# First transformer block on one core: the pool projections and the first gates in another order

## The chip, the core and the metric

The kernel runs on one core of one Trainium2 chip. The metric is the device time of one execution in microseconds (us), as the median of the runs shown. The engines are TensorE (PE, its weight loads apart as PEld), VectorE (DVE), ScalarE (ACT), GpSimd (POOL) and the SyncE queue (SP), which issues DMAs.

## What is computed

Two transformer blocks in sequence on 512 tokens of width 1024, in float32. The change lies in the first one, whose mixer has two branches:

```python
z = u @ w_in[l]                       # pool part, q, k, v, two gates
win_sum = cs[:, 1:, sl] - cs[:, lo, sl]
outs.append(win_sum / count - pf[:, :, sl])      # per group, windows (2, 4, 8, 16)
y = jnp.einsum('bsgc,gcd->bsgd', y, pool_w)      # one 128x128 matrix per group
y = y.reshape(B, S, POOL_WIDTH) * pool_scale
y_pool = pool_mixer(p, pool_w[l], pool_scale[l]) @ w_branch_pool[l]
y_attn = moba_attention(q, k, v) @ w_branch_attn[l]
m = jax.nn.sigmoid(g_pool) * y_pool + jax.nn.sigmoid(g_attn) * y_attn
```

## The kernel before

All activations lie transposed, 128 features by 512 tokens a tile. A float32 product is made of three matmuls of rounded parts: weight high by input high (L397), weight high by input low (L401), weight low by input high (L405). So each weight block of 128x128 costs three matmuls of 512 columns, and each operand is made in two steps: a high part (ACT, `round`, L293, or L285 for weights) and the rest, the low part (POOL, L245 or L241 for weights, or DVE, L500).

The order of every engine is written out ahead of time by a planner (`Flow.run`, L907). One generator, the main line, yields the large products one after another; beside it processes wait for events that the planner reckons with its own clock (attention heads, evacuations, products of the pool). When nothing beside the main line is ripe on TensorE, the next step of the main line is issued, so the projections fill the gaps between the heads: they are the fillers of the change's name. `linear` (L1033) issues the steps of one projection: with G tiles at a time, K = 8 input tiles, G x 8 x 3 matmuls. Only where the main line itself has no step that can be issued (`yield "idle"`) does the planner resume a process that isn't ripe; on the chip that is a wait in TensorE's row.

The names, in `first_block` (L1649):

- `w_p`, three tiles in a row: the projections of pool groups 1, 2 and 3 (group 0 is done with the first products of the block), 24 matmuls each. `pool_in(g)` (L1680) takes the result: evacuation from PSUM with the norm's factor (`scaled_out`, DVE, L646), g + 1 doublings that make a window's sum (`double`, DVE, L675 and the copy L676), the mean (`mean`, DVE, L681, L683, L684), high part on ACT (L293), low part on POOL (L245).
- `pool_product(g)` (L1744): three matmuls (L483, L484, L485) with the group's matrix, the scale (DVE, L691), high part (ACT, L293), low part (DVE, L500). The matrices come with one DMA (`pool_weights`, L1732, L208).
- `w_gp` and `w_ga`: the gates of the pool and of the attention, here the first two tiles of each, 48 matmuls a pair; evacuated (L646) and put through a sigmoid (L347).
- `w_bp`: the branch product of the pool. It reads the results of groups 0, 1, 2, 3 in this order, six matmuls a group for two tiles. `w_ba` follows, the branch product of the attention.

In the kernel before the main line runs: the last q, k, v tiles, then `w_p` for groups 1, 2, 3, then `w_gp`, `w_ga`, then `w_bp`. The attention's last two heads (6 and 7) are issued among the `w_p` steps: `turn` (L427) transposes, `pv_halves` (L449, L454) products, on DVE `add_half` (L630) and `out_low` / `turn_low` (L639).

Of the kernel before, what the change touches and what calls it, by code (L numbers as in the profile page):

```python
# [140 lines left out]
class Machine:  # L141
# [32 lines left out]
    def hl(self, i):  # L174
        return self.ra[:, i, 0, :], self.ra[:, i, 1, :]

    def vc(self, name, i):
        return self.vec[:, V_COLS[name] + i:V_COLS[name] + i + 1]
# [669 lines left out]
class Schedule:  # L848
# [9 lines left out]
    def row(self, kind, *args):  # L858
        self.rows.append((kind, args))
        self.begun.append(self.time_of(args))  # L860
        return len(self.rows) - 1
# [12 lines left out]
    def done(self, engine, name, key):  # L874

        n = key[0] if isinstance(key, tuple) else key
        kind, args = self.rows[n]
        start = max(self.clock[engine], self.begun[n] + 0.06)
        took = duration(kind, engine, args)
        self.begun[n] = self.ended[(name, key)] = start + took  # L880
        self.clock[engine] = start + max(0.06, took - (0.0 if engine in ("pe", "gp") else 0.09))
        self.last[engine] = (self.m.sig(name), key)
        return self.last[engine]
# [53 lines left out]
def build(sc, m, A, out):  # L937
# [45 lines left out]
    def next_unit(name, idx):  # L983
        u = st["used"]
        st["used"] += 1
        if u % 2 == 0:
            sc.units.append((name, idx // 2))
        if plan is None:
            return u, WS[u % NU], None
        assert plan[u // 2] == (name, idx // 2), (plan[u // 2], name, idx)  # L990
        while st["split"] < min(total, u + 1 + min(LOOK, 1 + u)):
            put_split(st["split"])
            st["split"] += 1
        return u, unit_slot(u), unit_tok[u]
# [9 lines left out]
    def banks_of(lb, n):  # L1004

        if None in [bank_free[b] for b in lb[:n]]:
            return None
        bs = [rot(lb) for _ in range(n)]
        freed = tuple(tuple(bank_free[b]) for b in bs)
        for b in bs:  # L1010
            bank_free[b] = None
        return bs, freed
# [10 lines left out]
    def multiply(unit, places, x, freed, start, stop, evac=None):  # L1023

        u, parts, split_done = unit
        xh, xl, xt = x
        n = row("mm", parts, split_done, (xh, xl), high_of(xt), tuple(xt), places, freed, start, stop)
        unit_used[u] = done("pe", "mm", (n, len(places) - 1))
        if stop:
            for j, (b, _) in enumerate(places):  # L1030
                evac(j, b, (m.sig("mm"), (n, j)))

    def linear(name, G, K, rhs, ntiles, evac, lb, first=0):  # L1033

        kk = 4 // G
        base = first * K // 4
        for g in range(ntiles // G):
            got = banks_of(lb, G)
            while got is None:
                yield "idle"  # L1040
                got = banks_of(lb, G)
            bs, freed = got
            for ku in range(K // kk):
                unit = next_unit(name, base + g * (K // kk) + ku)
                for q in range(kk):
                    k = ku * kk + q
                    while rhs(k) is None:
                        yield "idle"
                    places = tuple((b, (q * G + j) * 128) for j, b in enumerate(bs))
                    multiply(unit, places, rhs(k), freed, k == 0, k == K - 1,  # L1050
                             lambda j, b, t: evac(first + g * G + j, b, t))
                    freed = ()
                    yield
# [35 lines left out]
    def parts_of(dst, src, made, eng, free, tell, scale=1.0):  # L1089

        dh, dl = dst
        yield 0, "ac", lambda: (*made, *free())
        hi = done("ac", "high", row("round", dh, src, tuple(made), tuple(free()), scale))
        yield 0, eng, lambda: (hi,)
        n = row("rest", dl, dh, src, hi, eng)
        tell(done("ve", "low_v", n) if eng == "v" else done("gp", "low_p", n))
# [21 lines left out]
    def rhs_of(x):  # L1118
        return lambda k: (*x["slots"][k], x["tok"][k]) if x["tok"][k] else None
# [45 lines left out]
    def scaled(x, b, tok, need=3):  # L1165

        yield 0, "v", lambda: (tok, x["rb"]) if x["rb"] and len(T.free) >= need else None
        i, z, free = T.get()
        v = done("ve", "evac", row("scaled_out", z, b, x["rb"], free, tok))
        bank_free[b] = stat["rb_use"] = (v,)  # L1170
        return i, z, v
# [81 lines left out]
    LB3 = [0, 1, STB]  # L1253
# [395 lines left out]
    def first_block():  # L1649
# [9 lines left out]
        rhs_u = rhs_of(u)  # L1659
# [20 lines left out]
        def pool_in(g):  # L1680
            def process(b, tok):
                i0, x, v = yield from scaled(u, b, tok, 5)
                yield 0, "v", lambda: (v,) if len(T.free) > 3 else None
                (i1, y1, f1), (i2, y2, f2) = T.get(), T.get()
                src, dst, oth, free = x, y1, y2, (*f1, *f2)
                for r in range(g + 1):
                    yield 0, "v", lambda: (v,)
                    v = done("ve", "elem_v", row("double", dst, src, 1 << r, v, free))
                    src, dst, oth, free = dst, oth, dst, ()
                yield 0, "v", lambda: (v,)  # L1690
                v = done("ve", "elem_v", row("mean", dst, src, x, g, v))

                def tell(y):
                    for i in (i0, i1, i2):
                        T.release(i, y)
                    p_in[g] = (y,)
                yield from parts_of(hl(PY + g), dst, (v,), "p", tuple, tell)
            return lambda _, b, tok: launch(process(b, tok))
# [21 lines left out]
        for j in range(1, 4):  # L1720
            gate = lambda j=j: j < 2 or 2 * j - 3 in heads_used
            for name, ev in (("w_q", qk_tile(j, 0, qs(j))), ("w_k", qk_tile(j, 1, None)),
                             ("w_v", v_tile(u, VV + j % 2, ("v", j), gate))):
                yield from linear(name, 1, 8, rhs_u, 1, ev, lb, first=j - 1)
                if lb[-1] == 5:
                    lb = LB2
        yield from linear("w_p", 1, 8, rhs_u, 3, lambda j, b, t: pool_in(j + 1)(0, b, t), LB3)

        pw_parts = hl(PT1 + 2)
        pw_tok = []  # L1730
# [13 lines left out]
        def pool_product(g):  # L1744
            yield 0, "pe", lambda: (*pw_tok, *p_in[g], *bank_free[LB7[0]]) if (
                pw_tok and g in p_in and T.free and bank_free[LB7[0]] is not None) else None
            b = rot(LB7)
            n = row("pool_mm", pw_parts, slice(128 * g, 128 * g + 128), hl(PY + g), b, (*bank_free[b], *pw_tok, *p_in[g]))
            t = done("pe", "mm", (n, 0))
            bank_free[b] = None  # L1750
            i, z, free = T.get()
            yield 0, "v", lambda: (t,)
            v = done("ve", "evac", row("pool_scale", z, b, g, t, free))
            bank_free[b] = (v,)

            def tell(y):
                T.release(i, y)
                pool_done[g] = (y,)
            yield from parts_of(hl(PY + g), z, (v,), "v", lambda: (t,), tell)
# [5 lines left out]
        def evac_g(base):  # L1765
            def f(j, b, tok):
                def process():
                    i, z, v = yield from scaled(u, b, tok, 4)
                    yield 0, "ac", lambda: (v,)
                    sg[(base, j)] = (i, z, done("ac", "act", row("sigmoid", z, vc("b_gate", base + j), v)))  # L1770
                launch(process())
            return f
# [28 lines left out]
        launch(pool_weights())  # L1801
        for g in range(4):
            launch(pool_product(g))
        yield from linear("w_gp", 2, 8, rhs_u, 2, evac_g(0), LB3, first=0)
        yield from linear("w_ga", 2, 8, rhs_u, 2, evac_g(8), LB3, first=0)
        while 7 not in heads_used:
            yield "idle"
        t_heads = now("pe")
# [467 lines left out]
    def whole():  # L2276
        u = yield from first_block()
        u = yield from second_block_diff(u)
        u, back = yield from ffn2(0, u, U_B, ("attn", 8))
        u = yield from second_block_sliding(u, back)  # L2280
        yield from ffn2(1, u, None, None)
# [127 lines left out]
```

## Time and profile before

| | |
|---|---|
| Median of 3 runs | 1958.52 us (1957.97 to 1958.56) |
| The profiled execution, its own time | 1956.75 us |
| Its span, first to last instruction | 1954.9 us |
| TensorE busy | 1930.3 us, 99% |
| DVE / ACT / POOL busy | 1176.4 / 923.8 / 1107.9 us |
| TensorE idle with a named releaser | 18.9 us in eleven kinds of wait, the longest 7.5 us at the start |
| Mean granted clock of TensorE | 0.997 |

The profiled execution lies 1.85 us above its span and 1.77 us below the median. TensorE is busy nearly all the time, so what a change does is read from the places where TensorE has nothing to issue, from the wait that ends last there, and from the granted clock behind such a place. A granted clock of 1.00 is 2.4 GHz, 0.50 is 1.2 GHz. Most stalls of the whole program are a microsecond or less.

### The profile page before, as it was taken

What the parts mean: (1) busy time and instruction counts of PE and PEld (TensorE: products, weight loads), DVE (VectorE), ACT (ScalarE), POOL (GpSimd) and SP (SyncE); (2) the same over time, 40 slices, a digit from 0 to 9 for tenths busy, and PEclk for the clock granted to TensorE, in tenths of its full rate; (3) what the DMA queues carried; (4) which work ended last, traced back from release to release, by engine and by line L of the source; (5) the groups of instructions that cost most, each with busy time, mean ns of one, the idle gap of its engine ahead of it and who ended that gap; (6) DMA issues with size and microseconds to landing.
All of it is one profiled execution on the core that took longest, in us unless ns stands there. A gap on an engine that the chain in (4) does not pass through costs nothing.

```text
span 1954.9 us, 25157 instructions
## 1 busy us (share of the span) xinstructions
PE 1930.3 (99%) x9200; PEld 1589.6 (81%) x9200; DVE 1176.4 (60%) x1978; ACT 923.8 (47%) x1752; POOL 1107.9 (57%) x848
## 2 busy tenths in 40 slices
PE   8999999999999999999999999999999999999998
PEld 6878888888888887777888888888787888888887
DVE  6773325353433488776774746756688775746755
ACT  5644336533333366554543443445577543433443
POOL 5335544454444457554675666664874576656653
PEclk9999999999999999999999999999999999999999
DMA  4122233233232332112323322323211323222321
GB/s 170 57 71 97 95 110 129 95 105 103 97 111 97 101 105 76 54 55 70 128 94 108 98 86 97 108 87 108 72 44 33 130 98 103 98 91 97 99 95 65
DMA packets 53705, 182.71 MB, mean 93 GB/s; under 512 B 5840, under 2 KB 8272, under 8 KB 53584
## 3 DMA queue, kind: packets, MB, share of 16 engines
q1 hardware_dynamic: 53584, 181.12, 28.0%
q8 instruction: 73, 1.20, 0.3%
q14 instruction: 48, 0.39, 0.1%
HBM read 174.80 MB, written 6.29 MB: 93 GB/s over the span
## 4 chain that ended last, share of the span: by engine, by line
PE 96%; DVE 3%; ACT 0%; issue 0%; DMA 0%; SPq 0%; DVEq 0%; ACTq 0%
PE b L397 29%; PE b L405 29%; PE b L401 29%; PE b L427 3%; PE b L417 1%; PE b L454 1%; PE b L465 1%; PE b L449 1%; PE b L420 1%; PE b L421 1%; PE b L475 0%; PE b L434 0%; PE b L440 0%; PE b L441 0%; DVE ra L639 0%
## 5 line engine op out<-in xcount | busy, mean ns | idle before, releaser
L241 POOL TENSOR_TENSOR ra<-raw,ra 128x512 fp32r<-128x512 f32 x632 | 876.5, 1395 | 756.9 <-ACT ra L285 755.3
L397 PE MATMUL b<-ra 128*128 128x512 f32 (+1 forms) x2560 | 890.2, 392 | 11.0 <-ACT ra L285 7.5
L405 PE MATMUL b<-ra 128*128 128x512 f32 (+1 forms) x2560 | 877.0, 387 | 0.0
L401 PE MATMUL b<-ra 128*128 128x512 f32 (+1 forms) x2560 | 876.7, 387 | 0.0
L285 ACT ACTIVATE ra<-raw 128x512 fp32r<-128x512 f32 x632 | 392.0, 628 | 521.9 <-PE b L405 513.4
L397 PEld LDWEIGHTS b<-ra 128*128 128x128 f32 x2560 | 480.9, 188 | 109.8 <-issue 10.6
L405 PEld LDWEIGHTS b<-ra 128*128 128x128 f32 x2560 | 481.0, 188 | 98.9
L401 PEld LDWEIGHTS b<-ra 128*128 128x128 f32 x2560 | 482.0, 188 | 94.0 <-DVE ra L500 0.4
L755 DVE TENSOR_TENSOR h<-b,h 128x512 f32<-128x512 f32 x136 | 91.5, 682 | 56.1 <-PE b L405 55.5
L646 DVE TENSOR_TENSOR tmp<-b,rb 128x512 f32<-128x512 f32 x66 | 45.2, 690 | 109.4 <-PE b L405 109.1
L639 DVE TENSOR_TENSOR ra<-b,ra 128x512 fp32r<-128x512 f32 (+4 forms) x166 | 92.1, 566 | 22.3 <-ACT ra L336 20.3
L646 DVE TENSOR_TENSOR gbuf<-b,rb 128x512 f32<-128x512 f32 x50 | 34.2, 689 | 99.0 <-PE b L405 99.0
L336 ACT ACTIVATE ra<-b 128x512 fp32r<-128x512 f32 (+3 forms) x142 | 66.6, 487 | 49.6 <-PE b L427 48.5
L725 DVE TENSOR_TENSOR fa<-b,fa 128x512 f32<-128x512 f32 x56 | 38.6, 688 | 78.8 <-PE b L405 78.8
L293 ACT ACTIVATE ra<-tmp 128x512 fp32r<-128x512 f32 x83 | 51.2, 627 | 57.2 <-DVE tmp L774 25.6
L500 DVE TENSOR_TENSOR ra<-tmp,ra 128x512 fp32r<-128x512 f32 x65 | 67.1, 1048 | 4.3 <-ACT ra L293 3.8
L330 ACT ACTIVATE fa<-fa,sm 128x257 f32<-128x257 f32 (+4 forms) x96 | 53.4, 558 | 23.7 <-DVE sm L617 23.3
L427 PE MATMUL b<-ident,fa 128*128 128x128 f32 x368 | 59.9, 278 | 2.8 <-DVE ra L639 2.7
L427 PEld LDWEIGHTS b<-ident,fa 128*128 128x128 f32 x368 | 41.8, 141 | 15.8 <-DVE ra L639 5.8
L592 DVE TENSOR_REDUCE sm<-b 128x1 f32<-128x512 f32 x64 | 39.8, 681 | 18.8 <-PE b L421 18.7
L506 DVE SCALAR_TENSOR_TENSOR ra<-h,vec,ra 128x512 fp32r<-128x512 f32 x40 | 44.5, 1118 | 9.0 <-ACT ra L298 9.0
L617 DVE CUSTOM_DVE_ANT_0 fa<-b,mask 128x257 f32<-128x257 f32 (+4 forms) x96 | 43.6, 486 | 6.0 <-PE b L421 5.6
(277 smaller groups left out, 1806.7 us busy)
## 6 DMA issues: line engine op xcount, KB each, us to landing
raw<-in_f_g SPq DMA_DIRECT2D x40, 512.0 KB, 3.4
raw<-in_f_v SPq DMA_DIRECT2D x40, 512.0 KB, 3.5
raw<-in_f_d SPq DMA_DIRECT2D x40, 512.0 KB, 3.4
raw<-in_w_up SPq DMA_DIRECT2D x32, 512.0 KB, 3.5
raw<-in_w_down SPq DMA_DIRECT2D x32, 512.0 KB, 3.4
raw<-in_p_g SPq DMA_DIRECT2D x16, 512.0 KB, 3.4
raw<-in_w_gp SPq DMA_DIRECT2D x8, 512.0 KB, 3.5
raw<-in_w_ga SPq DMA_DIRECT2D x8, 512.0 KB, 3.5
```

What stands on the lines that cost most here:

```text
L241: e.tensor_tensor(wl, src, wh.bitcast(F), ALU.subtract).then_inc(*w_low.mark(n))
L285: e.activation(wh, src, ACT.Copy).then_inc(*w_high.mark(n))
L330: e.activation(p, p, ACT.Exp, bias=nm, scale=-1.0, accum_out=su).then_inc(*soft.mark(n))
L336: e.activation(dst, src, ACT.Copy).then_inc(*high.mark(n))
L397: e.matmul(m.banks[b][:, 0:xh.shape[-1]], wh[:, c:c + 128], xh, start=start, stop=False)
L401: e.matmul(m.banks[b][:, 0:xh.shape[-1]], wh[:, c:c + 128], xl, start=False, stop=False)
L405: last = e.matmul(m.banks[b][:, 0:xh.shape[-1]], wl[:, c:c + 128], xh, start=False, stop=stop)
L427: x = e.transpose(m.banks[b][:, 128 * q:128 * q + 128], src[:, 128 * q:128 * q + 128], m.ident[:, :])
L500: e.tensor_tensor(dl, src, dh.bitcast(F), ALU.subtract).then_inc(*low.mark(n))
L639: e.tensor_tensor(dl, src, dh.bitcast(F), ALU.subtract).then_inc(*low.mark(n))
L646: e.tensor_tensor(z, banks[b][:, :], m.rb[:, :], ALU.mult).then_inc(*evac.mark(n))
L755: e.tensor_tensor(dst, src, hk, ALU.add).then_inc(*evac.mark(n))
```

## The change

The three tiles of `w_p` are no longer yielded in a row. Group 3 comes first, then the two gate tiles of `w_gp`, then group 2, then the two gate tiles of `w_ga`, then group 1, and then the main line goes on to `w_bp`. The processes of `pool_weights` and `pool_product` are launched ahead of the three tiles instead of behind them. Nothing is added or left out: each engine does the same operations on the same shapes.

```diff
                 yield from linear(name, 1, 8, rhs_u, 1, ev, lb, first=j - 1)
                 if lb[-1] == 5:
                     lb = LB2
-        yield from linear("w_p", 1, 8, rhs_u, 3, lambda j, b, t: pool_in(j + 1)(0, b, t), LB3)
...
         launch(pool_weights())
         for g in range(4):
             launch(pool_product(g))
-        yield from linear("w_gp", 2, 8, rhs_u, 2, evac_g(0), LB3, first=0)
-        yield from linear("w_ga", 2, 8, rhs_u, 2, evac_g(8), LB3, first=0)
+        for g in (3, 2, 1):
+            yield from linear("w_p", 1, 8, rhs_u, 1, lambda j, b, t: pool_in(j + 1)(0, b, t), LB3, first=g - 1)
+            if g > 1:
+                yield from linear(("w_ga", "w_gp")[g - 2], 2, 8, rhs_u, 2, evac_g((8, 0)[g - 2]), LB3, first=0)
```

How the rows of the engines move. A row is a line of the kernel, the operation, what it writes and reads (`b0` to `b7` are the PSUM banks, `ra` holds operands in high and low parts, `tmp` and `gbuf` are scratch tiles), its size, and in brackets the signals that it waits for: `evac` an evacuation on DVE, `mm` a product of TensorE, `high` a high part on ACT, `low_p` and `low_v` a low part on POOL and on DVE, `w_high` and `w_low_p` the two parts of weights.

TensorE before, where the last projection of `w_p` ends (bank b7, group 3):

```order
L397 MATMUL b7<-ra 128x512
L401 MATMUL b7<-ra 128x512
L405 MATMUL b7<-ra 128x512
L397 MATMUL b0<-ra 128x512 [waits evac,w_high]
L401 MATMUL b0<-ra 128x512
L405 MATMUL b0<-ra 128x512 [waits w_low_p]
L397 MATMUL b1<-ra 128x512 [waits evac]
```

Behind it stand the 96 matmuls of the gates, from b0 and b1 on, and only then the first product of the pool.

TensorE now, just behind the last matmul of the last projection (bank b0, group 1); b3 and b4 are the two tiles of `w_bp`, L483 to L485 on b5 the pool's product of group 1:

```order
L397 MATMUL b3<-ra 128x512 [waits high,w_high]
L401 MATMUL b3<-ra 128x512 [waits low_v]
L405 MATMUL b3<-ra 128x512 [waits w_low_p]
L397 MATMUL b4<-ra 128x512
L401 MATMUL b4<-ra 128x512
L405 MATMUL b4<-ra 128x512
L483 MATMUL b5<-ra 128x512 [waits low_p]
L484 MATMUL b5<-ra 128x512
L485 MATMUL b5<-ra 128x512
L397 MATMUL b3<-ra 128x512 [waits high]
L397 MATMUL b4<-ra 128x512
L401 MATMUL b3<-ra 128x512 [waits low_v]
```

Between the end of a projection and a row that needs its result there stand six matmuls where there were 96 and more.

DVE before, the chain of group 1 (from its first doubling on), then the attention's `add_half`:

```order
L675 TENSOR_TENSOR gbuf<-tmp 128x511 [waits evac,low_p]
L676 COPY gbuf<-tmp 128x1
L675 TENSOR_TENSOR gbuf<-gbuf 128x510 [waits elem_v]
L676 COPY gbuf<-gbuf 128x2
L681 TENSOR_TENSOR gbuf<-gbuf,vec 128x16 [waits elem_v]
L683 TENSOR_TENSOR gbuf<-gbuf,tmp 128x16 [waits elem_v]
L684 SCALAR_TENSOR_TENSOR gbuf<-gbuf,tmp 128x496
L630 TENSOR_TENSOR b6<-b6,ssq 64x512 [waits act]
```

DVE now, the same chain of group 1 with what stands ahead of and behind it:

```order
L500 TENSOR_TENSOR ra<-gbuf,ra 128x512 [waits high]
L500 TENSOR_TENSOR ra<-tmp,ra 128x512 [waits high]
L646 TENSOR_TENSOR tmp<-b0,rb 128x512 [waits low_p,mm]
L675 TENSOR_TENSOR tmp<-tmp 128x511 [waits evac]
L676 COPY tmp<-tmp 128x1
L675 TENSOR_TENSOR tmp<-tmp 128x510 [waits elem_v]
L676 COPY tmp<-tmp 128x2
L681 TENSOR_TENSOR tmp<-tmp,vec 128x16 [waits elem_v]
L683 TENSOR_TENSOR tmp<-tmp 128x16 [waits elem_v]
L684 SCALAR_TENSOR_TENSOR tmp<-tmp 128x496
L691 TENSOR_SCALAR gbuf<-b5,vec 128x512 [waits low_v,mm]
L500 TENSOR_TENSOR ra<-gbuf,ra 128x512 [waits high]
```

The chain of group 1 has moved behind the attention and behind the products of groups 2 and 3, whose low parts are the two rows ahead of it; its own product's scale and low part stand right behind it.

DVE now, at the place where the chain of group 1 stood before: the doublings of group 3 (third and fourth), with the last heads' rows among them:

```order
L675 TENSOR_TENSOR gbuf<-gbuf 128x508 [waits elem_v]
L676 COPY gbuf<-gbuf 128x4
L630 TENSOR_TENSOR b6<-b6,ssq 64x512 [waits act]
L675 TENSOR_TENSOR gbuf<-gbuf 128x504 [waits elem_v]
L676 COPY gbuf<-gbuf 128x8
L639 TENSOR_TENSOR ra<-b2,ra 128x128 [waits high]
L639 TENSOR_TENSOR ra<-b3,ra 128x2x128 [waits high]
L639 TENSOR_TENSOR ra<-b4,ra 128x3x128 [waits high]
L639 TENSOR_TENSOR ra<-b5,ra 128x4x128 [waits high]
```

Two doublings and two copies more stand ahead of the low parts of head 7, and the mean now behind them.

## Rows read from the trace of the kernel before

**Rows 1.** The page: busy us (share of the span) and instructions of each engine.

```profile
PE 1930.3 (99%) x9200; PEld 1589.6 (81%) x9200; DVE 1176.4 (60%) x1978; ACT 923.8 (47%) x1752; POOL 1107.9 (57%) x848
```

**Rows 2.** Waits of TensorE, whole span: us in total, times, longest.

```profile
PE b L397 <- ACT ra L285: 7.5, 1, 7.5
PE b L427 <- DVE ra L639: 2.7, 3, 1.8
PE b L397 <- DVE tmp L646: 2.0, 1, 2.0
...
PE b L397 <- ACT gbuf L353: 0.4, 1, 0.4
PE b L397 <- DVE gbuf L646: 0.2, 1, 0.2
```

**Rows 3.** A stretch: length; busy us of PE, PEld, DVE, ACT, POOL; clock; DMA.

```profile
160.00:170.00 10.00, 10.00 (x45) 7.99 (x44) 6.33 (x10) 4.60 (x8) 3.85 (x3) 1.00 0.15 52
```

**Rows 4.** TensorE timeline, group 1's projection ends: start us, us, row.

```profile
121.73 0.40 PE L405 MATMUL b<-ra 128*128 128x512 f32 x1
```

**Rows 5.** DVE timeline, group 1's chain.

```profile
122.16 0.69 DVE L646 TENSOR_TENSOR tmp<-b,rb 128x512 f32<-128x512 f32 x1
122.96 0.92 DVE L675 TENSOR_TENSOR gbuf<-tmp 128x511 f32<-128x511 f32 x1
...
123.97 0.69 DVE L675 TENSOR_TENSOR gbuf<-gbuf 128x510 f32<-128x510 f32 x1
124.58 0.16 DVE L676 COPY gbuf<-gbuf 128x2 f32<-128x2 f32 x1
...
125.08 0.67 DVE L684 SCALAR_TENSOR_TENSOR gbuf<-gbuf,tmp 128x496 f32<-128x496 f32 x1
```

**Rows 6.** ACT and POOL timelines, the end of group 1's chain.

```profile
125.97 0.65 ACT L293 ACTIVATE ra<-gbuf 128x512 fp32r<-128x512 f32 x1
...
126.70 1.29 POOL L245 TENSOR_TENSOR ra<-gbuf,ra 128x512 fp32r<-128x512 f32 x1 [3.37 <-ACT ra L293]
```

**Rows 7.** TensorE, ACT and DVE timelines, products of the pool, then `w_bp`.

```profile
159.20 0.39 PE L485 MATMUL b<-ra 128*128 128x512 f32 x1
...
161.47 0.39 PE L397 MATMUL b<-ra 128*128 128x512 f32 x1
161.82 0.50 PE L401 MATMUL b<-ra 128*128 128x512 f32 x1
...
160.41 1.32 ACT L293 ACTIVATE ra<-tmp 128x512 fp32r<-128x512 f32 x2
...
161.07 0.69 DVE L500 TENSOR_TENSOR ra<-tmp,ra 128x512 fp32r<-128x512 f32 x1
```

**Rows 8.** Timelines at the stall of 2 us: DVE, then TensorE.

```profile
111.74 0.68 DVE L646 TENSOR_TENSOR tmp<-b,rb 128x512 f32<-128x512 f32 x1
...
112.56 0.52 PE L397 MATMUL b<-ra 128*128 128x512 f32 x1 [2.01 <-DVE tmp L646]
```

**Rows 9.** Stretches of 2 us behind that stall, columns as Rows 3.

```profile
112.00:114.00 2.00, 1.44 (x5) 1.11 (x6) 1.93 (x5) 0.67 (x3) 1.28 (x1) 0.71 0.01 4
114.00:116.00 2.00, 2.00 (x10) 1.23 (x8) 0.78 (x2) 0.60 (x1) 0.00 (x0) 0.50 0.00 0
116.00:118.00 2.00, 2.00 (x11) 1.48 (x10) 1.75 (x6) 1.11 (x4) 0.00 (x0) 0.94 0.00 0
```

**Rows 10.** DVE and POOL timelines, doublings of group 3 beside POOL.

```profile
139.42 1.60 DVE L675 TENSOR_TENSOR tmp<-tmp 128x510 f32<-128x510 f32 x1
140.95 1.25 DVE L676 COPY tmp<-tmp 128x2 f32<-128x2 f32 x1
...
139.10 1.37 POOL L241 TENSOR_TENSOR ra<-raw,ra 128x512 fp32r<-128x512 f32 x1 [3.76 <-ACT ra L285]
```

**Rows 11.** DVE and TensorE timelines, last heads' low parts and head 7's product.

```profile
126.39 2.27 DVE L639 TENSOR_TENSOR ra<-b,ra 128x128 fp32r<-128x128 f32 x5
...
129.09 0.74 PE L449 MATMUL b<-ra 128*128 128x512 f32 x4
```

## The prediction, as it stood before the changed kernel ran

> **What bounds the kernel now.** I began with the busy times of the page: TensorE is busy 1930.3 us, 99% [rows 1], so an edit that adds or removes no work can change the time only where TensorE stands still or runs at the lower clock. Next I read the waits of TensorE over the whole span: eleven kinds, 18.9 us in all, led by the 7.5 us at the start [rows 2]. Only two lie near the rows that the change moves: one of 2.0 us and one of 0.2 us, both behind an evacuation (L646). Then came the stretches of time around it: where the products of the pool and `w_bp` follow the gates, TensorE is busy without a break, at a granted clock of 1.00 [rows 3]. So the old order loses 0.2 us there and nothing else; what is to be gained is that, and the question is whether the new order keeps TensorE fed.
>
> The stall of 2.0 us ends at 112.56 us [rows 8]. It belongs to the first row of the first `w_p` tile, which takes the bank that the last v tile has just filled. That row stands in the same place now (the two orders part only behind the first `w_p` tile), so this stall and its clock stay.
>
> **The change part by part.** All matmuls of 512 columns below are counted at 0.227 us from start to start: ten of them lie between 159.20 and 161.47 us [rows 7].
>
> *What goes.* In the old order a gate tile's bank is freed only by the evacuation of the previous tile, which is the 0.2 us [rows 2]. Now 24 matmuls of `w_p` (5.4 us) stand between the gates and the next use of their banks, so 0.2 us goes.
>
> *Head 7.* Its product on TensorE waits for low parts on DVE, and two more doublings and copies of group 3 and its mean now stand ahead of the last of them. In the old order the four low parts and the first head's `out_low` take 2.27 us from 126.39 [rows 11]. Two doublings with their copies add 2 x (0.69 + 0.16) = 1.7 us [rows 5] while the mean merely changes its side, so DVE ends near 128.7 + 1.7 = 130.4. Nine more matmuls stand ahead of head 7's product (9 x 0.227 = 2.0 us), so it comes up at 129.09 + 2.0 = 131.1 [rows 11]. With 0.14 us from DVE to TensorE [rows 8] that is a cover of 0.6 us: price nothing. If POOL slows one of the two doublings (below) the cover is gone and up to 1 us is paid.
>
> *The products of groups 0, 2 and 3.* Group 0's takes the bank that group 2's projection leaves, six matmuls behind its end: 7 x 0.227 = 1.59 us after the start of the last one. An evacuation of that kind ends 0.43 + 0.69 us after that start [rows 4, 5], and TensorE starts 0.14 us after an evacuation's end [rows 8]: 1.26 us, a cover of 0.3 us. DVE must be free for it; nothing but an earlier gate's evacuation stands ahead. Group 2's low part has 57 matmuls (12.9 us) to come; group 1's whole chain took 6.3 us, and one doubling, a scale and a low part more are under 3 us by rows of their kind [rows 5, 7]. Group 3 has longer still. Price nothing for all of them. The DMA of the pool's matrices moves up on SP with the launch, between two weight loads, and its splitting still waits for gates' matmuls: nothing waits for it in either order.
>
> *Group 1, the last.* Its projection is now the last thing ahead of `w_bp`, whose first six matmuls need group 0 alone; then TensorE's row is the product of group 1, which waits for the low part on POOL. The trace shows this chain whole, at a time when TensorE had other work. The last matmul starts at 121.73 [rows 4], the evacuation at 122.16, the mean ends at 125.75 [rows 5], ACT makes the high part from 125.97 and POOL the low part from 126.70 to 127.99 [rows 6]. With 0.14 us to TensorE that is 6.40 us from the last matmul's start. TensorE has that matmul and six more to issue, 1.59 us, and then stands still for 4.8 us. Two parts of this were contention: the first doubling took 0.92 us, the second 0.69 us [rows 5]; and ACT began 0.22 us after the mean [rows 6]. In the new place the head's work is over, DVE has two low parts ahead that are long due, and POOL has no row in between but a weight split that TensorE's first half of the tile releases. Without both it is 4.4 us. I take 4.5.
>
> Then the result of group 1 is needed at once, by the next six matmuls of `w_bp`. In the old trace group 0's product starts its last matmul at 159.20; ACT's high part is ready when DVE's L500 begins, at 161.07, and the low part lets L401 go at 161.82 [rows 7], 2.62 us after that start. There three other products and more stood in between; now nothing does. Taking off the matmul itself and the two L397 that need the high part alone, 2.62 - 3 x 0.227 = 1.9 us of standing still, in two pieces.
>
> *The clock.* Behind the stall of 2.01 us the granted clock falls to its lower level, 1.2 GHz: 0.71, 0.50 and 0.94 in the three stretches of 2 us from 112 on [rows 9]. The clock that is missing is (0.29 + 0.50 + 0.06) x 2 = 1.7 us of TensorE's time. The stall here is longer and followed by a second one after three matmuls, so I expect one such fall, 1.7 us. The bounds: 0.3 us, if most of the low time falls into the second stall, and 3.4 us, if each stall brings its own.
>
> A rule speaks against that term: the Trainium skill, TensorE: Matmul & The Clock Gate, section "What's actually happening", says that for modelling the ramp costs under 1% of a typical span and should not be fitted. Here that would be under 19.5 us, so this trace's 1.7 us agrees with it, and yet it is a fifth of the sum. By the rule, taken as leaving the term out, the sum would be 6.2 us.
>
> *The sum.* 4.5 + 1.9 + 1.7 - 0.2 = 7.9 us. None of it is hidden: with TensorE at 99%, what it loses in one place comes on top. The profiled execution took 1956.75 us, 1.77 us below the median, so it would go to 1964.7 us; on the median of 1958.52 I forecast **1966.4 us**, 0.4% slower.
>
> **The rivals.** *More than that: the chain is slowed by POOL, or the clock falls twice.* For group 3 the second doubling took 1.60 us and its copy 1.25 us while POOL was busy, against 0.69 and 0.16 us [rows 5, 10]: 2.0 us more. With both, 7.9 + 2.0 + 1.7 = 11.6 us, 1970.1 us; with one of them 1968 us. It needs POOL busy in the 3.5 us after the projection's end; the order shows one weight split that could slip there. The Trainium skill says the same of the cause: GPSIMD Engine Reference, section "1. Specifications", has POOL's SBUF interfaces shared with VectorE, contending with instructions of two SBUF inputs. The doubling agrees (1.60 us beside POOL), and the rule alone would not tell which of the two cases holds here.
>
> *Less: the clock costs nothing beyond the stalls.* 4.4 + 1.65 + 0.3 - 0.2 = 6.2 us, 1964.7 us, if the low clock lies in the second stall and that is shortened to its wait for the high part. For it: the two stalls are 0.7 us apart. Against it: the stall of 2.01 us was followed by a fall that lay wholly in busy time [rows 8, 9].
>
> *Not slower: later waits swallow it.* Of the waits of TensorE, those behind 160 us sum to 8.4 us in seven kinds, from L427 behind DVE's L639, 2.7 us, to L397 behind ACT's L353, 0.4 us [rows 2]. If what they wait for were not put off by the stall, 7.9 us could be given back and the time would stay at 1958.5 us. It decides from the point where the releasers depend on DMA or on work that runs ahead of TensorE. All the named ones are DVE, ACT and POOL rows that work on TensorE's own results, so they move along with it. I see no gain beyond the 0.2 us.
>
> **How the numbers follow.** The forecast case (6.5 to 9.5 us) gets 0.73, the larger loss 0.12, the smaller 0.08 and the swallowed one 0.04; 0.03 is left for something smaller that I don't see, such as half the chain covered (4 us). The range leaves out the top of the first rival and the swallowed case: 1963.5 to 1970.0 us. A comparison of this kernel tells about 0.2%, 3.9 us, from no change. Slower by more than that: 0.94; within it: 0.05; faster: 0.01.
>
> **What would show it.** Right: in the waits of TensorE a new L483 behind POOL's L245 of about 4.5 us near 161 us, then L397 behind ACT's L293 of about 1.7 us and a short L401 behind DVE's L500, and a granted clock of 0.5 to 0.7 behind them; the waits of 0.2 us gone; all later waits the same. Wrong: no wait at L483, which would mean that the group's low part was ready, or the same wait with less idle time later in the program.

## The result, and the profile after

The changed kernel takes 1965.66 us (median of 5 runs, 1965.08 to 1967.65) against 1958.51 us for the kernel before: ratio 1.0039, 95% interval 1.0028 to 1.0051. That is 7.15 us by the medians, 5.5 to 10.0 us by the interval. The forecast was 7.9 us, 1966.4 us.

The busy times of the page, the line that answers to [rows 1]: all engines do what they did before within 4 us, and the span, 1963.6 us, has grown. DVE has one instruction less and POOL one more: behind the change the planner reckons the rest of the program anew, and an addition of squares that DVE did at 702 us is done by POOL at 711 us (L250 runs 20 times instead of 19). So the engines don't do quite the same operations as before; the place of the change itself is not touched by it.

```profile
PE 1933.8 (98%) x9200; PEld 1592.6 (81%) x9200; DVE 1176.7 (60%) x1977; ACT 923.6 (47%) x1752; POOL 1106.4 (56%) x849
```

The waits of TensorE over the whole span (us in total, times, longest), against [rows 2]: two new ones, L483 behind POOL and L397 behind ACT's L293. The 2.0 us behind L646's `tmp` stayed; the 0.2 us behind its `gbuf` is not in the list any more.

```profile
PE b L483 <- POOL ra L245: 4.0, 1, 4.0
...
PE b L397 <- DVE tmp L646: 2.0, 1, 2.0
...
PE b L397 <- ACT ra L293: 1.5, 1, 1.5
```

TensorE's timeline there (start us, us, row, in brackets the idle time before it and its releaser). The first line is the last matmul of group 1's projection, the second the last of the six that `w_bp` can do with group 0.

```profile
161.50 0.39 PE L405 MATMUL b<-ra 128*128 128x512 f32 x1
...
162.86 0.39 PE L405 MATMUL b<-ra 128*128 128x512 f32 x1
167.26 0.79 PE L483 MATMUL b<-ra 128*128 128x512 f32 x1 [4.02 <-POOL ra L245]
167.86 0.63 PE L484 MATMUL b<-ra 128*128 128x512 f32 x1
168.28 0.63 PE L485 MATMUL b<-ra 128*128 128x512 f32 x1
170.42 1.22 PE L397 MATMUL b<-ra 128*128 128x512 f32 x2 [1.50 <-ACT ra L293]
...
174.72 0.40 PE L397 MATMUL b<-ra 128*128 128x512 f32 x1
```

The same stretch on DVE, then ACT, then POOL: what [rows 5, 6] showed under the cover of other work is now the only thing that runs.

```profile
161.93 0.69 DVE L646 TENSOR_TENSOR tmp<-b,rb 128x512 f32<-128x512 f32 x1 [1.93 <-PE b L405]
162.65 0.69 DVE L675 TENSOR_TENSOR tmp<-tmp 128x511 f32<-128x511 f32 x1
...
163.44 0.69 DVE L675 TENSOR_TENSOR tmp<-tmp 128x510 f32<-128x510 f32 x1
...
164.54 0.67 DVE L684 SCALAR_TENSOR_TENSOR tmp<-tmp 128x496 f32<-128x496 f32 x1
...
165.24 0.63 ACT L293 ACTIVATE ra<-tmp 128x512 fp32r<-128x512 f32 x1 [4.93 <-DVE tmp L684]
169.74 0.63 ACT L293 ACTIVATE ra<-gbuf 128x512 fp32r<-128x512 f32 x1 [3.86 <-DVE gbuf L691]
...
165.95 1.26 POOL L245 TENSOR_TENSOR ra<-tmp,ra 128x512 fp32r<-128x512 f32 x1 [3.55 <-ACT ra L293]
```

And in stretches of 2 us (length; busy us of PE, PEld, DVE, ACT, POOL; clock; DMA), where [rows 3] had a clock of 1.00 throughout:

```profile
166.00:168.00 2.00, 0.73 (x2) 0.64 (x3) 0.00 (x0) 0.00 (x0) 1.21 (x1) 0.68 0.00 0
168.00:170.00 2.00, 0.91 (x3) 0.19 (x1) 0.75 (x1) 0.27 (x1) 0.00 (x0) 0.50 0.00 0
170.00:172.00 2.00, 1.58 (x4) 1.25 (x5) 0.69 (x1) 0.88 (x2) 1.04 (x1) 0.50 0.00 0
172.00:174.00 2.00, 2.00 (x7) 1.57 (x6) 0.00 (x0) 0.56 (x1) 0.23 (x1) 0.62 0.35 76
174.00:176.00 2.00, 2.00 (x10) 1.62 (x9) 0.39 (x1) 0.07 (x1) 1.29 (x1) 1.00 0.47 186
```

**What the stretch lost.** From 161.50 to 174.72 us TensorE starts 22 matmuls (six, three and twelve behind the first). At 0.227 us each these take 5.0 us; they took 13.2. So 8.2 us went here: 167.26 - 162.86 - 0.23 = 4.2 us ahead of the product, 1.5 us behind it as the profile counts it, 0.2 us ahead of L401, and the rest, 2.3 us, as matmuls that stood 0.42 us and more apart at the lower clock. The 0.2 us is in the timeline of the weight loads (PEld), not in the list of TensorE's waits:

```profile
171.14 0.63 PEld L401 LDWEIGHTS b<-ra 128*128 128x128 f32 x2 [0.23 <-DVE ra L500]
```

Against it stand the 0.2 us that went and 0.4 us behind ACT's L353 in a later part of the program [rows 2], which is missing from the list after: 7.6 us. By the starts of the matmuls around them these two small waits cost the kernel before 0.5 and 0.7 us, which leaves 7.0 us.

The profiled span grew by 8.7 us, about 1.5 us more than the medians of the runs: rows ahead of the change's place already come later (the evacuation of group 1's place in [rows 5], at 122.16, has its counterpart at 123.60), and the wait at the start is 7.8 us instead of 7.5. That part is the profiled execution's, not the change's: a short wait of TensorE that every version has early on (L417 behind DVE's `sm`) ends anywhere from 46.42 to 48.59 us in the traces of this document, and from there to the stall of 2.0 us all versions that have this stall take the same 65.4 us. So a fairer measure is the long stretch from that wait to another one that every version has, in the kernel before:

```profile
47.15 0.49 PE L417 MATMUL b<-ra 64*128 64x512 f32 x1 [0.76 <-DVE sm L617]
...
924.89 0.47 PE L397 MATMUL b<-ra 128*128 128x512 f32 x1 [0.88 <-DVE h L755]
```

It took 877.7 us before and takes 884.6 us now, from 48.59 to 933.22: 6.9 us more.

### The profile page after: what moved, and what is told of

Its sections match the earlier page's. It is cut to its first block, busy times and chain, and to the rows that moved or that the text cites. A ratio compares the mean times of both kernels' runs of the same rounds, so it can differ in the third digit from the quotient of the medians.

```text
span 1963.6 us, 25163 instructions
## 1 busy us (share of the span) xinstructions
PE 1933.8 (98%) x9200; PEld 1592.6 (81%) x9200; DVE 1176.7 (60%) x1977; ACT 923.6 (47%) x1752; POOL 1106.4 (56%) x849
## 4 chain that ended last, share of the span: by engine, by line
PE 97%; DVE 2%; issue 0%; DMA 0%; ACT 0%; POOL 0%; SPq 0%; DVEq 0%
PE b L397 29%; PE b L405 29%; PE b L401 29%; PE b L427 3%; PE b L417 1%; PE b L454 1%; PE b L465 1%; PE b L449 1%; PE b L420 1%; PE b L421 1%; PE b L475 0%; PE b L434 0%; PE b L440 0%; PE b L441 0%; DVE ra L639 0%
## 5 line engine op out<-in xcount | busy, mean ns | idle before, releaser
L397 PE MATMUL b<-ra 128*128 128x512 f32 (+1 forms) x2560 | 891.0, 393 | 12.2 <-ACT ra L285 7.8
L401 PE MATMUL b<-ra 128*128 128x512 f32 (+1 forms) x2560 | 877.4, 387 | 0.0
L397 PEld LDWEIGHTS b<-ra 128*128 128x128 f32 x2560 | 481.6, 189 | 110.9 <-issue 10.6
L401 PEld LDWEIGHTS b<-ra 128*128 128x128 f32 x2560 | 482.4, 188 | 93.8 <-DVE ra L500 0.2
L646 DVE TENSOR_TENSOR tmp<-b,rb 128x512 f32<-128x512 f32 x68 | 46.6, 690 | 150.7 <-PE b L405 150.5
L293 ACT ACTIVATE ra<-tmp 128x512 fp32r<-128x512 f32 x76 | 47.2, 628 | 49.6 <-DVE tmp L774 18.9
L646 DVE TENSOR_TENSOR gbuf<-b,rb 128x512 f32<-128x512 f32 x48 | 33.0, 689 | 56.2 <-PE b L405 56.2
L427 PE MATMUL b<-ident,fa 128*128 128x128 f32 x368 | 60.5, 280 | 2.8 <-DVE ra L639 2.7
L500 DVE TENSOR_TENSOR ra<-tmp,ra 128x512 fp32r<-128x512 f32 x58 | 59.5, 1036 | 6.1 <-ACT ra L293 5.8
L293 ACT ACTIVATE ra<-gbuf 128x512 fp32r<-128x512 f32 x61 | 38.2, 627 | 42.0 <-DVE gbuf L774 20.2
L427 PEld LDWEIGHTS b<-ident,fa 128*128 128x128 f32 x368 | 42.1, 142 | 15.8 <-DVE ra L639 5.8
```

Source lines behind the costliest of these rows:

```text
L293: e.activation(dst, src, ACT.Copy).then_inc(*high.mark(n))
L397: e.matmul(m.banks[b][:, 0:xh.shape[-1]], wh[:, c:c + 128], xh, start=start, stop=False)
L401: e.matmul(m.banks[b][:, 0:xh.shape[-1]], wh[:, c:c + 128], xl, start=False, stop=False)
L427: x = e.transpose(m.banks[b][:, 128 * q:128 * q + 128], src[:, 128 * q:128 * q + 128], m.ident[:, :])
L500: e.tensor_tensor(dl, src, dh.bitcast(F), ALU.subtract).then_inc(*low.mark(n))
L646: e.tensor_tensor(z, banks[b][:, :], m.rb[:, :], ALU.mult).then_inc(*evac.mark(n))
```

## The experiments

My theory: the price is the chain of the last projection (TensorE, DVE, ACT, POOL, TensorE), less the matmuls that TensorE has at hand meanwhile, then the same behind the product, and the clock that such a stall brings. The main rival: the new place of the gates, POOL's contention, or the new order in itself costs the time. Times are set against the kernel before on the same chip, by the ratio; "over" is (ratio - 1) x 1958 us, with the 95% interval in brackets. The last column is the long stretch between the two waits named above, against the 877.7 us of the kernel before; it is one execution each, but free of what happens at the program's start and end.

| kernel | us | over the kernel before | the long stretch |
|---|---|---|---|
| e1_gate_last | 1960.27 | +2.3 (0.8 to 4.1) | +2.0 |
| e2_group3_last | 1965.83 | +8.6 (6.1 to 11.4) | +8.3 |
| e3_no_gates_between | 1961.19 | +3.3 (1.8 to 5.1) | +3.8 |
| e5_spin | 1962.45 | +5.3 (3.3 to 7.2) | +4.9 |
| e8_ba_first | 1960.55 | +2.5 (0.8 to 4.3) | +0.8 |
| e10_bp_group1_last | 1963.21 | +5.7 (3.5 to 7.6) | +6.0 |
| e11_ba_first_group1_last | 1956.66 | -1.0 (-2.7 to +0.8) | -1.4 |
| e6_bank | 1957.54 | -0.2 (-2.0 to +1.6) | +0.7 |
| e12_all_and_bank | 1955.17 | -2.2 (-3.9 to -0.4) | -4.1 |

### e1_gate_last: the second gates behind the last projection

```diff
-            if g > 1:
-                yield from linear(("w_ga", "w_gp")[g - 2], 2, 8, rhs_u, 2, evac_g((8, 0)[g - 2]), LB3, first=0)
+            if g in (3, 1):
+                yield from linear("w_gp" if g == 3 else "w_ga", 2, 8, rhs_u, 2, evac_g(0 if g == 3 else 8), LB3, first=0)
```

> Order here: projection of group 3, the pool's first gates, group 2, group 1, and only then the attention's first gates (48 matmuls, 10.9 us) ahead of w_bp. Theory (the loss is the chain of the last projection, which nothing covers, its product's chain behind it, and the clock that falls in the waits): all three go, no wait at L483, 1958.3 us (1957.5 to 1960). Rival (it costs time to put gates ahead of projections, since their evacuations and sigmoids stand in the queues of DVE and ACT and hold scratch tiles): half of the loss stays, 1961 us or more.

Measured: +2.3 us. Most of the loss goes when 48 matmuls of `w_ga` stand behind the last projection, as the theory has it. What is left shows in TensorE's timeline as small waits at three products, with the clock at 1.00 behind each:

```profile
149.09 0.50 PE L483 MATMUL b<-ra 128*128 128x512 f32 x1 [0.22 <-DVE gbuf L646]
...
151.01 0.50 PE L483 MATMUL b<-ra 128*128 128x512 f32 x1 [0.96 <-POOL ra L245]
...
156.66 0.50 PE L483 MATMUL b<-ra 128*128 128x512 f32 x1 [0.60 <-POOL ra L245]
```

All three are new. The 0.22 us is not that of [rows 2]: there a gate waits for a bank, here a product waits for the bank of group 1's projection, whose evacuation stands on DVE behind group 2's mean:

```profile
147.76 0.67 DVE L684 SCALAR_TENSOR_TENSOR tmp<-tmp 128x496 f32<-128x496 f32 x1
148.35 0.68 DVE L646 TENSOR_TENSOR gbuf<-b,rb 128x512 f32<-128x512 f32 x1
149.14 0.69 DVE L675 TENSOR_TENSOR gbuf<-gbuf 128x511 f32<-128x511 f32 x1
```

The forecast (no loss, 1957.5 to 1960 us) was missed by these: with groups 2 and 1 back to back their chains queue on DVE, group 2's product comes 24 matmuls earlier in TensorE's order, and POOL's low parts take longer there (1.78 and 1.66 us, against 1.29 and 1.26 in the changed kernel). The rival's figure, half of the loss, lies inside the interval, but none of the three waits is one for a gate's evacuation or sigmoid.

### e3_no_gates_between: the projections in the new order, in a row

```diff
         for g in (3, 2, 1):
             yield from linear("w_p", 1, 8, rhs_u, 1, lambda j, b, t: pool_in(j + 1)(0, b, t), LB3, first=g - 1)
-            if g > 1:
-                yield from linear(("w_ga", "w_gp")[g - 2], 2, 8, rhs_u, 2, evac_g((8, 0)[g - 2]), LB3, first=0)
+        yield from linear("w_gp", 2, 8, rhs_u, 2, evac_g(0), LB3, first=0)
+        yield from linear("w_ga", 2, 8, rhs_u, 2, evac_g(8), LB3, first=0)
```

> Order here: groups 3, 2, 1 in a row, then both pairs of gates: the half of the change that turns the order of the means, without the other half. Theory: cover of 96 matmuls behind the last chain, 1958.3 us (1957.5 to 1960), as before. Rival (the longest chain first stands among the last heads' rows on DVE and puts them off): a wait at L449 or L427 and 1960 us or more.

Measured: +3.3 us, nearer to the rival's figure than to mine. But it shows no wait at L449 or L427, as the rival has it, and none for group 1: TensorE waits once, at the first product, for the low part of the pool's matrices (the wait, then stretches with columns as in those of the changed kernel):

```profile
139.66 0.47 PE L483 MATMUL b<-ra 128*128 128x512 f32 x1 [2.76 <-DVE ra L500]
```

```profile
140.00:142.00 2.00, 2.00 (x8) 1.53 (x7) 1.90 (x4) 0.00 (x0) 0.94 (x1) 0.65 0.41 168
142.00:144.00 2.00, 2.00 (x6) 1.62 (x5) 2.00 (x5) 1.58 (x3) 0.46 (x1) 0.50 0.00 0
```

L500 starts at 138.83 there, behind group 2's doublings on DVE, two of which take 1.81 and 1.74 us beside POOL. So it matters how early the first product stands in TensorE's order: here right behind the projections, 30 matmuls ahead of its place in the changed kernel and 96 ahead of that in the kernel before, it comes up while DVE is still at these doublings. Whether that place comes from the products' earlier launch or from the planner's clock no run separates. In the changed kernel the gates between the projections keep DVE's row short, and no product but the last waits.

### e2_group3_last: the order turned round

```diff
-        for g in (3, 2, 1):
+        for g in (1, 2, 3):
...
-            if g > 1:
-                yield from linear(("w_ga", "w_gp")[g - 2], 2, 8, rhs_u, 2, evac_g((8, 0)[g - 2]), LB3, first=0)
+            if g < 3:
+                yield from linear(("w_gp", "w_ga")[g - 1], 2, 8, rhs_u, 2, evac_g((0, 8)[g - 1]), LB3, first=0)
```

> Order here: group 1, pool's gates, group 2, attention's gates, group 3, so the last chain has four doublings instead of two. Theory (the length of the last chain sets the wait): two doublings with their copies more, 2 x (0.69 + 0.16) = 1.7 us; the wait at L483 grows from 4.0 to 5.7 us, the time from 1965.7 to 1967.4 us (1966.5 to 1968.5). Rival (the price is one of the place alone, the wait for the product and the clock): 1965.7 us, unchanged. Rival (the order from the longest mean down is what costs): faster than 1965.

Measured: +8.6 us, with the interval across both figures; the trace decides. The wait at L483 did not grow, 4.04 us, but not for the rival's reason. The chain did get longer, and by more than I expected: the first doubling took 1.82 us beside a weight split of POOL. TensorE, however, had 18 matmuls of `w_bp` at hand and not six, since `w_bp` takes the groups in the order 0 to 3 and only group 3 was missing. Rows of DVE, POOL and TensorE:

```profile
161.75 1.82 DVE L675 TENSOR_TENSOR tmp<-tmp 128x511 f32<-128x511 f32 x1
...
161.74 1.29 POOL L241 TENSOR_TENSOR ra<-raw,ra 128x512 fp32r<-128x512 f32 x1 [0.23 <-ACT ra L285]
...
169.11 0.80 PE L483 MATMUL b<-ra 128*128 128x512 f32 x1 [4.04 <-POOL ra L245]
```

Two more doublings with their copies (1.7 us) and 1.1 us of contention are 2.8 us more; 12 x 0.227 = 2.7 us is the longer cover. I had left the cover out. It suggested the next experiments: lengthen the cover alone.

The waits are thus those of the changed kernel, 4.0 and 1.5 us, and yet the long stretch is 1.4 us longer than the changed kernel's. The rest is the clock's: here it stays at 0.50 to 178 us, where in the changed kernel it is back at 1.00 from 174 us on (columns as in the stretches of the changed kernel):

```profile
176.00:178.00 2.00, 2.00 (x6) 1.54 (x6) 0.22 (x1) 0.16 (x1) 1.27 (x1) 0.50 0.00 0
```

### e10_bp_group1_last: `w_bp` takes group 1 last

```diff
-            yield from linear("w_bp", 2, 4, rhs_p, 2, evac_bp, LB7, first=2 * jj)
+            yield from linear("w_bp", 2, 4, rhs_p, 2, evac_bp, LB7, first=2 * jj, late=1 if jj == 0 else None)
```

`late` makes `linear` take the input tiles in the order 0, 2, 3, 1.

> The changed kernel, but the first w_bp takes the groups as 0, 2, 3, 1, so that 18 matmuls and not 6 stand ahead of group 1's product. Theory: the wait at L483 shrinks by 12 x 0.227 = 2.7 us, from 4.0 to 1.3 us, the wait of 1.5 us behind the product stays; without a fall of the clock 2.6 us over the kernel before (1960.6 on a median of 1958), with one of 1.7 us 4.3 us (1962.3). Rival (the wait is set by something that moves along with TensorE, a transfer or a weight split): the wait at L483 stays at about 4 us and the time at 7 us over the kernel before, 1965.

Measured: +5.7 us, and the wait at L483 is 2.43 us, not 1.3. Again the first doubling ran beside a weight split (1.82 us instead of 0.69, 1.1 us more), which explains the difference: 12 matmuls less, 1.1 us more. Rows of DVE, POOL and TensorE:

```profile
161.55 1.82 DVE L675 TENSOR_TENSOR tmp<-tmp 128x511 f32<-128x511 f32 x1
...
161.53 1.29 POOL L241 TENSOR_TENSOR ra<-raw,ra 128x512 fp32r<-128x512 f32 x1 [0.23 <-ACT ra L285]
...
167.29 0.50 PE L483 MATMUL b<-ra 128*128 128x512 f32 x1 [2.43 <-POOL ra L245]
...
169.76 0.80 PE L397 MATMUL b<-ra 128*128 128x512 f32 x1 [1.51 <-ACT ra L293]
```

Here the clock is still 1.00 at the product and falls only with the second stall; then twelve matmuls from 169.76 to 175.35 us take 5.6 instead of 2.7 us, the short wait for the product's low part included.

### e8_ba_first and e11_ba_first_group1_last: other work as cover

```diff
-            yield from linear("w_bp", 2, 4, rhs_p, 2, evac_bp, LB7, first=2 * jj)
-            yield from linear("w_ba", 2, 4, rhs_o1, 2, evac_ba, LB7, first=2 * jj)
+            two = (("w_bp", rhs_p, evac_bp), ("w_ba", rhs_o1, evac_ba))
+            for name, rhs, ev in two if jj else two[::-1]:
+                yield from linear(name, 2, 4, rhs, 2, ev, LB7, first=2 * jj)
```

e11 has this and the order 0, 2, 3, 1 in the first `w_bp`.

> The changed kernel, but in the first output block w_ba (24 matmuls on the attention's results, long ready) stands ahead of w_bp. Theory (the price is a chain without cover): 30 matmuls of 0.227 us, 6.8 us, now stand ahead of group 1's product instead of 6, more than the 5.8 us of the chain, so the wait of 4.0 us at L483 is gone and the wait of 1.5 us behind the product's high part stays; does the clock fall behind 1.5 us? With no fall 1.2 to 1.5 us over the kernel before (1959.5 on a median of 1958), with a fall as behind the stall of 2.0 us 3 us over it (1961). Rival (the gates' new place, POOL or the order itself costs the time): 7 us over it stays, 1965.

> The changed kernel with both: w_ba ahead of the first w_bp, and group 1 last in that w_bp. The product of group 1 can then go out as soon as its low part is there, and 12 matmuls (2.7 us) of groups 2 and 3 stand behind it, more than the 1.5 to 1.9 us for the result's high and low parts. Theory: no wait of TensorE between 150 and 175 us, clock 1.00 there, and the time within 0.5 us of the kernel before (1958). Rival (something of the change costs apart from these two waits and their clock): 2 us or more over it, 1960 or more.

Measured: e8 +2.5 us, e11 -1.0 us. In e8 the wait at L483 is gone and the 1.5 us behind the product stay, with a short wait of L401's weight load and a clock of 1.00 (TensorE and its weight loads, then stretches as length, PE busy, clock, DMA):

```profile
170.10 0.74 PE L397 MATMUL b<-ra 128*128 128x512 f32 x2 [1.51 <-ACT ra L293]
...
170.83 0.30 PEld L401 LDWEIGHTS b<-ra 128*128 128x128 f32 x2 [0.43 <-DVE ra L500]
```

```profile
168.00:170.00 2.00, 0.60 (x3) 1.00 0.00 0
170.00:172.00 2.00, 1.90 (x7) 1.00 0.00 0
```

The interval of e8 holds both of its forecasts, with a fall of the clock and without; the clock in the trace settles that there was none, in this execution.

In e11 neither is there: no wait of TensorE between 114 and 300 us. The groups still come as 3, 2, 1 with the gates between them, and the loss is gone, so the order of the change costs nothing but its last chain; the rival falls.

### e5_spin: matmuls without use in both waits

```diff
+            if g == 1:
+                row("spin", pw_parts[0], hl(PY)[0], 6, 18)
             n = row("pool_mm", pw_parts, slice(128 * g, 128 * g + 128), hl(PY + g), b, (*bank_free[b], *pw_tok, *p_in[g]))
...
+            if g == 1:
+                row("spin", pw_parts[0], hl(PY)[0], 6, 7)
```

> The changed kernel with matmuls whose results nobody reads, into a free bank: 18 ahead of the product of group 1 and 7 behind it, 4.1 and 1.6 us at full clock, so that TensorE works through both waits. Theory (the clock falls because TensorE stands still, and that costs about 2.0 us on top of the waits): the granted clock stays at 1.00, 1963.7 us (1963 to 1964.5), 2.0 us under the changed kernel. Rival (the low clock lies in the waits and costs nothing): 1965.7 us. Rival (the matmuls without use push the product back): above 1965.7 us.

The 25 matmuls write a bank that nobody reads. Measured: +5.3 us. TensorE loses the stalls' time here as well, to work without use, but the clock is 1.00 in every stretch from 150 to 176 us (columns as above):

```profile
166.55 0.50 PE L487 MATMUL b<-ra 128*128 128x512 f32 x1
...
167.34 1.77 PE L481 MATMUL b<-ra 128*128 128x512 f32 x7
169.02 0.73 PE L397 MATMUL b<-ra 128*128 128x512 f32 x2
```

(The first row is the product, L487 in this kernel; L481 are the matmuls without use.) From the last useful matmul at 162.10 to the next of `w_bp` at 169.02 it is 6.9 us; four matmuls of use are 0.9 of it, so 6.0 us are lost, against 8.2 us in the changed kernel. The clock's part is 2.2 us by the traces, 7.6 - 5.3 = 2.3 us by the two ratios, though their intervals overlap, and 6.9 - 4.9 = 2.0 us by the long stretch. The traces settle that the clock falls in the one and not in the other; the size rests on them more than on the times.

### e6_bank and e12_all_and_bank: the old stall at 112 us

```diff
+        LB3[:] = [1, STB, 0]
```

> The kernel before with one line added: the list of banks is turned ahead of w_p, so that the first w_p tile doesn't take the bank that the last v tile has just filled. Theory: the stall of 2.0 us at 112 us goes, and with it the 1.7 us that the low clock behind it costs: 3.7 us less than the kernel before, 1954.3 on a median of 1958. Rival (the clock's fall there is not the stall's): 2.0 us less, 1956; or the next tile's bank becomes the wait: no change.

> The changed kernel with w_ba ahead of the first w_bp, group 1 last in that w_bp, and the list of banks turned ahead of w_p, so that the first w_p tile doesn't take the bank that the last v tile has just filled. In the kernel before with the turned list alone the 2.0 us at 112 us went and 1.8 us came back at the first product of the pool, whose matrices' high part stands on ACT behind group 3's mean. Here group 3's mean is over before those matrices come. Theory: neither wait, nor one at group 1's product; 3.5 us less than the kernel before, 1954.7 on a median of 1958.2. Rival (TensorE, running 3.7 us ahead, meets another part that isn't ready, since the doublings and POOL stay as slow as they are): a new wait of 1 to 2 us at one of the products (L483), and a time within 1 us of the kernel before.

e6 measured -0.2 us: no gain. The stall of [rows 8] is gone and the clock is 1.00 from 110 to 124 us, so the fall there was the stall's. But TensorE met the pool's matrices unready, and the clock fell behind that (TensorE's waits, then stretches as length, PE busy, clock, DMA):

```profile
115.29 0.52 PE L427 MATMUL b<-ident,fa 128*128 128x128 f32 x3 [0.45 <-DVE sm L596]
...
144.93 0.47 PE L483 MATMUL b<-ra 128*128 128x512 f32 x1 [1.83 <-DVE ra L500]
```

```profile
146.00:148.00 2.00, 2.00 (x6) 0.50 0.00 0
148.00:150.00 2.00, 2.00 (x8) 0.71 0.17 39
```

Their high part stands on ACT in row behind that of group 3, whose mean ends at 142.9 us after two doublings of 1.6 us beside POOL. It isn't that TensorE is early. With the turned list the planner writes another order: the first product of the pool stands 60 matmuls further up than in the kernel before, where it comes behind all the gates and needs no wait:

```profile
158.75 0.39 PE L483 MATMUL b<-ra 128*128 128x512 f32 x1
```

In the kernel before the matrices' low part is made from 147.06 us on, so at e6's place in the order, which TensorE reaches at 144.7 us there, the product would have had to wait as well. The edit thus took one stall away and, by the order that came with it, made another 33 us on. In e12 the turned list moves the products of groups 0, 2 and 3 up as well, by 18 to 48 matmuls against e11, but group 3 is long done by then and none of them waits; with the cover of e11 the end is free too: e12 measured -2.2 us, the only version here whose interval lies below the kernel before. Its waits of TensorE between 100 and 300 us come down to one:

```profile
114.69 0.52 PE L427 MATMUL b<-ident,fa 128*128 128x128 f32 x3 [0.43 <-DVE sm L596]
```

By the account it gains 2.0 + 1.7 us of stall and clock, less the 0.4 us of this wait, and the 0.5 and 0.7 us of the two small waits that went: 4.5 us. The long stretch is 4.1 us shorter. The times show less of it, 0.4 to 3.9 us; what takes the difference lies outside that stretch or in the spread of the runs, and is open.

## Why the prediction was right, step by step

- **The wait for group 1 (4.5 us):** 4.2 us, 4.0 as the profile counts it, just under the lower bound of 4.4. The chain from the last matmul's start took 5.76 us, where the forecast's 4.5 us stand for 6.1; the first doubling took 0.69 us and ACT began as the mean ended. It was the uncontended end of the bounds; e2 and e10 show the contended one, 1.1 us more, when a weight split falls beside the first doubling. The Trainium skill, GPSIMD Engine Reference, section "1. Specifications", has GpSimd's SBUF interfaces shared with VectorE; the 1.82 us against 0.69 us agree.
- **Behind the product (1.9 us in two pieces):** 1.7 us, 1.5 at the high part against 1.65 and 0.2 at the low part against 0.25. At full clock, in e8, the second piece is 170.83 - 170.10 - 2 x 0.227 = 0.3 us; the lower clock of the two matmuls ahead of it covers part of it in the changed kernel.
- **The clock (1.7 us):** 2.0 to 2.3 us, the term that was mis-sized most. One fall was forecast, with the size of the old stall's; it came as one, but lasted from the product's three matmuls past the second stall. The rival that has it free (6.2 us) fell: e5 shows what is left without it. The Trainium skill, TensorE: Matmul & The Clock Gate, section "What's actually happening", puts the ramp penalty under 1% of a typical kernel's span, with the advice not to fit a count of cold matmuls; 2.3 of 1964 us agrees, and yet it is about 30% of this change's loss.
- **The sum (7.9 us): the errors offset, which is luck.** 0.3 and 0.2 us too much for the waits, 0.3 to 0.6 too little for the clock, and a gain at L353 that the forecast didn't have. The path, the two waits and one fall of the clock, came as forecast.
- **Head 7 (no price, cover 0.6 us):** no wait. Its last low part ends on DVE at 132.02 and its product on TensorE starts at 132.55, so with the 0.14 us from DVE to TensorE the cover was 0.4 us.
- **The products of groups 0, 2 and 3 (no price):** they start at 144.73, 156.29 and 156.97 us without a wait in the changed kernel. e3 and e6 show the price of the row that I passed over as free, the matrices' low part: up to 2.8 us, once the first product stands that early in TensorE's order.
- **Later waits swallow it:** none of the seven did, but for the 0.4 us at L353. The 0.4 us are in the lists of the kernel before, e1, e3 and e6, and in none of the others; the same four have the addition of squares on DVE, the others on POOL. In the changed kernel the matmul at that place no longer waits for ACT's copy: it starts while the copy is being made (TensorE, then ACT):

```profile
700.47 0.39 PE L397 MATMUL b<-ra 128*128 128x512 f32 x1
...
700.31 0.64 ACT L353 ACTIVATE gbuf<-b 128x512 f32<-128x512 f32 x1
```

So the 0.4 us go with an order that the planner reckoned anew; what tipped it is not settled.

## What to carry to other kernels

Work that is put last pays for its whole chain through the other engines, less the matmuls that TensorE has at hand and that don't depend on it; count both, since a change of order can lengthen the chain and its cover at once (e2). A stall taken away only pays if what the next rows need is ready where the new order puts them: the same line of code gave nothing in e6, where it also drew a product forward into a wait, and helped in e12. Where a planner writes the order, look at the order that an edit brings and not at the edit alone. To cover a chain, move independent work behind it, as `w_ba` in e11, rather than reorder the chain's own steps.

## What the runs showed of the hardware

- Stalls of 0.60, 0.96 and, in e8, 1.5 us left the granted clock at 1.00. Those of 1.83 (e6), 2.0 [rows 8, 9], 2.8 (e3) and 4.0 us were followed by matmuls at 0.50, and in e10 the fall came only with a second stall of 1.5 us, 0.7 us of work behind one of 2.4 us. The length alone doesn't decide: a stall of 1.8 us that every version has late in the program (L427 behind DVE's `ra`, at 1505.25 us in the kernel before) was followed by 0.50 in eight of the eleven traces, and left the clock at 1.00 in e2, e5 and e10.
- Matmuls without use, issued into the stalls, kept the clock at 1.00 there and gave back some 2 us (e5).
- One weight split on POOL beside a doubling of 128x511 on DVE makes it 1.82 us instead of 0.69, while POOL's own row stays at 1.29 us (e2, e10). In e1 POOL's row is slowed as well: a low part of 1.78 us beside a doubling of 128x510 that takes 1.57 us.
